# Token norms whose square roots, reciprocals and spreads go in two halves of the columns, and modulation columns and coefficients placed elsewhere

## What is computed

```python
def rms_norm(x, g):
    y = xf * lax.rsqrt(jnp.mean(xf * xf, axis=-1, keepdims=True) + EPS)
    return (y * g.astype(jnp.float32)).astype(x.dtype)
...
    mod = c_act @ ada_w[i] + ada_b[i]
    sh1, sc1, g1, sh2, sc2, g2 = [m[:, None, :] for m in jnp.split(mod, N_MOD, axis=-1)]
    h = rms_norm(x, mix_pre_g[i]) * (1.0 + sc1) + sh1
    y = hybrid_mixer(h, ...)                      # attention with forgetting, and a gated convolution
    x = x + g1 * rms_norm(y, mix_post_g[i])
    h = rms_norm(x, ffn_pre_g[i]) * (1.0 + sc2) + sh2
    y = swiglu_ffn(h, w_ffn_in[i], w_ffn_out[i])
    x = x + g2 * rms_norm(y, ffn_post_g[i])
...
    h = _modulate(x, norm_g[i], shift, scale)     # second block: a Mamba-2 mixer
    x = x + gate[:, None, :] * _mamba2_mixer(h, ...)
    hk = _modulate(x, kv_norm_g, kv_shift, kv_scale)
    ...                                           # then stick-breaking attention on keys and values of hk
    return _rmsnorm(x, final_g)
```

## Time and profile before

| | us |
|---|---|
| median of 3 runs | 1412.69 (1410.79 to 1412.97) |
| the profiled execution's own time | 1412.92 |
| its span in the trace | 1411.1 |
| TensorE busy (share of the span) | 1348.2 (96%) |
| VectorE busy | 823.5 (58%) |
| ScalarE busy | 588.5 (42%) |
| GpSimd busy | 407.2 (29%) |
| mean granted TensorE clock | 0.976 of 2.4 GHz |

### The profile page before, as it was taken

One profiled execution on the slowest core, in us unless ns is written; L12 is line 12 of the kernel. 1 busy time (PEld: TensorE's weight loads), 2 busy tenths in 40 slices (PEclk: granted clock), 3 DMA queues, 4 the chain that ended last, 5 costly groups with the idle time before them and its releaser, 6 DMA issues. The chain is left out here.

```text
span 1411.1 us, 19533 instructions
## 1 busy us (share of the span) xinstructions
PE 1348.2 (96%) x7904; PEld 1072.8 (76%) x7904; DVE 823.5 (58%) x965; ACT 588.5 (42%) x849; POOL 407.2 (29%) x191
## 2 busy tenths in 40 slices
PE   5999999799999999999999999999998999999996
PEld 3778867578888888887788876767776899777775
DVE  2789974566555564433757656778733822566544
ACT  4323656332222232113444456787522422455441
POOL 0000000149887888998100000000000050232310
PEclk9999999889999999999799999999999999999998
DMA  9434071124545536543222243334132432111121
GB/s 382 156 136 150 31 268 61 60 90 178 186 171 223 189 128 235 209 178 149 93 91 89 92 131 93 113 119 143 60 111 91 156 121 90 60 60 34 57 90 60
DMA packets 41350, 181.12 MB, mean 128 GB/s; under 512 B 3392, under 2 KB 20160, under 8 KB 21312
## 3 DMA queue, kind: packets, MB, share of 16 engines
q1 hardware_dynamic: 40128, 171.73, 33.9%
q10 hardware_dynamic: 1152, 8.39, 1.7%
HBM read 173.75 MB, written 6.36 MB: 128 GB/s over the span
## 5 line engine op out<-in xcount | busy, mean ns | idle before, releaser
L193 DVE TENSOR_TENSOR wlo<-raw,whi 128x2048 fp32r<-128x2048 f32 x95 | 257.4, 2710 | 169.2 <-ACT whi L189 166.6
L200 POOL TENSOR_TENSOR ada_raw<-ada_raw,cs 128x2048 f32<-128x2048 f32 x36 | 142.6, 3962 | 498.6 <-DVE h2lo L451 451.0
L271 PE MATMUL ps<-hhi,whi 128*128 128x512 f32 x640 | 252.1, 394 | 2.3 <-PEq L563 0.8
L271 PE MATMUL ps<-hhi,wlo 128*128 128x512 f32 x640 | 249.4, 390 | 0.0
L271 PE MATMUL ps<-hlo,whi 128*128 128x512 f32 x640 | 249.1, 389 | 0.0
L189 ACT ACTIVATE whi<-raw 128x2048 fp32r<-128x2048 f32 x95 | 181.5, 1911 | 143.6 <-PE ps L1312 91.3
L209 POOL TENSOR_TENSOR ada_raw<-ada_raw 128x1024 f32<-128x1024 f32 x72 | 166.0, 2305 | 5.6
L271 PEld LDWEIGHTS ps<-hhi,whi 128*128 128x128 f32 x640 | 120.2, 188 | 28.6 <-issue 2.4
L271 PEld LDWEIGHTS ps<-hhi,wlo 128*128 128x128 f32 x640 | 120.1, 188 | 25.6
L271 PEld LDWEIGHTS ps<-hlo,whi 128*128 128x128 f32 x640 | 120.3, 188 | 24.3
L2041 POOL TENSOR_TENSOR x<-x,rest 128x256 f32<-128x256 f32 (+3 forms) x32 | 49.0, 1532 | 160.2 <-DVE rest L2340 160.2
(11 more groups left out here) (374 smaller groups left out, 2781.1 us busy)
## 6 DMA issues: line engine op xcount, KB each, us to landing
raw<-panels SPq DMA_DIRECT2D x87, 1024.0 KB, 4.9
ada_raw<-ada SPq DMA_DIRECT2D x48, 1024.0 KB, 6.7
first<-ada SPq DMA_DIRECT2D x8, 1024.0 KB, 20.6
bc<-ac_rows SPq DMA_DIRECT2D x32, 256.0 KB, 3.7
raw<-panels ACTq DMA_DIRECT2D x8, 1024.0 KB, 5.0
x_kept<-x SPq DMA_DIRECT2D x2, 2048.0 KB, 9.7
x<-x_kept SPq DMA_DIRECT2D x2, 2048.0 KB, 7.7
x<-x_in SPq DMA_DIRECT2D x1, 2048.0 KB, 10.8
```

What stands on the lines that cost most here:

```text
L193: e.tensor_tensor(wlo[:, c % 2, :, :], raw[:, c % 2, :, :], whi[:, c % 2, :, :].bitcast(F32), ALU.subtract).then_inc(lo_split, 1)
L200: e.tensor_tensor(ada_raw[:, c % 2, :, :], ada_raw[:, c % 2, :, :], cs[:, which, :].unsqueeze(2).to_broadcast([P, KT, 256]), ALU.mult).the ...
L271: mm = e.matmul(ps[:, 2 * (qc % 2) + b, :], w[:, c % 2, 2 * k + b, :], src[part][:, k, :], **flags)
```

## The change

In `token_std` the square root is taken in two halves of the 128 columns, and so is the reciprocal in `token_rs`, each half with its own semaphore count. `spread` waits for both square roots, and then for one half's reciprocal at a time: it has 4 multiplications per half, 8 in all, whose moving operand has 64 columns. All seven norms use it. In `post2` the 13 pending columns are placed 4, 5, 1, 1, 2, 0 and not 3, 3, 1, 1, 2, 3. The two coefficients of the last block are computed at the end of VectorE's work in the Mamba part, after its fourth group's norm and ahead of the wait for `x` to come back.

```diff
+        TOKEN_HALVES = (slice(0, P // 2), slice(P // 2, P))
...
         def token_std(act, no, s, bank):
             act.wait_ge(*no("ss_used", (s + 1) * KT))
-            act.activation(rsq[:], ps[:, bank, 0:P], ACT.Sqrt, bias=eps[:, 0:1],
-                           scale=1.0 / D).then_inc(nsem["std_ready"], 1)
+            for h in TOKEN_HALVES:
+                act.activation(rsq[:, h], ps[:, bank, h], ACT.Sqrt, bias=eps[:, 0:1],
+                               scale=1.0 / D).then_inc(nsem["std_ready"], 1)
         def token_rs(dve, no, s):
-            dve.wait_ge(*no("std_ready", s + 1))
-            dve.reciprocal(rsq[:], rsq[:]).then_inc(nsem["rs_ready"], 1)
+            for i, h in enumerate(TOKEN_HALVES):
+                dve.wait_ge(*no("std_ready", 2 * s + i + 1))
+                dve.reciprocal(rsq[:, h], rsq[:, h]).then_inc(nsem["rs_ready"], 1)
         def spread(pe, no, s, bank):
-            pe.wait_ge(*no("rs_ready", s + 1))
-            for b in range(TB):
-                mm = pe.matmul(ps[:, bank, b * P:(b + 1) * P], ident[:, 32 * b:32 * b + 1].to_broadcast([P, P]), rsq[:],
-                               start=True, stop=True)
+            pe.wait_ge(*no("std_ready", 2 * s + 2))
+            for i, h in enumerate(TOKEN_HALVES):
+                pe.wait_ge(*no("rs_ready", 2 * s + i + 1))
+                for b in range(TB):
+                    mm = pe.matmul(ps[:, bank, b * P + h.start:b * P + h.stop],
+                                   ident[:, 32 * b:32 * b + 1].to_broadcast([P, P]), rsq[:, h], start=True, stop=True)
             mm.then_inc(nsem["spread"], 1)
...
+        def norm_coefs(dve, gain, sc, slot, k0=0, k1=KT):
+            dve.scalar_tensor_tensor(out=coef[:, slot, k0:k1], in0=m(sc)[:, k0:k1], scalar=1.0, in1=gain[:, k0:k1],
+                                     op0=ALU.add, op1=ALU.mult).then_inc(nsem["coef_ready"], 1)
...
-                post2 = post_norm("ffn_post", "g2", ..., last, late=(41, 54, sums, [3, 3, 1, 1, 2, 3]))
+                post2 = post_norm("ffn_post", "g2", ..., last, late=(41, 54, sums, [4, 5, 1, 1, 2, 0]))
...
                         group_rs(dve, 3)
                         norm_lo(dve, 3)
+                        norm_coefs(dve, v("kv_norm"), "kvsc", 1)
+                        norm_coefs(dve, v("norm2", KT, KT), "ssc", 2)
                         dve.wait_ge(x_back, 16)
...
                 def _(dve):
-                    pre3["coefs"](dve)
-                    pre4["coefs"](dve)
                     pre3["dve"](dve)
```

More of the change, by code:

```diff
@@ L342, in post_norm @@
             N = nsem
-            no = counting(bank_done=KT - 1, kept=KT, sq_ready=2 * KT, ss_used=2 * KT, std_ready=2, rs_ready=2, spread=2,
+            no = counting(bank_done=KT - 1, kept=KT, sq_ready=2 * KT, ss_used=2 * KT, std_ready=4, rs_ready=4, spread=2,
                           scaled=KT, x_new0=KT // 2, x_new1=KT // 2, coef_ready=1)
@@ L442, in coefs @@
             def coefs(dve, k0=0, k1=KT):
-                dve.scalar_tensor_tensor(out=coef[:, slot, k0:k1], in0=m(sc)[:, k0:k1], scalar=1.0, in1=gain[:, k0:k1],
-                                         op0=ALU.add, op1=ALU.mult).then_inc(N["coef_ready"], 1)
+                norm_coefs(dve, gain, sc, slot, k0, k1)
             def on_dve(dve, k0=0, k1=KT):
@@ L558, in build @@
             x_landed = sem("x_landed")
-            x0 = counting(sq_ready=KT, ss_used=KT, std_ready=1, rs_ready=1, spread=1)
+            x0 = counting(sq_ready=KT, ss_used=KT, std_ready=2, rs_ready=2, spread=1)
             head = pre_norm(v("mix_pre"), "sc1", "sh1", hhi, hlo, h0, ps[:, 7, :], parts=4)
@@ L1226, in build @@
                 last = co + COUNT["ffn_out"] - 1
-                post2 = post_norm("ffn_post", "g2", y_place[:, 0:KT, :], y_place[:, 8:11, :], last, late=(41, 54, sums, [3, 3, 1, 1, 2, 3]))
+                post2 = post_norm("ffn_post", "g2", y_place[:, 0:KT, :], y_place[:, 8:11, :], last, late=(41, 54, sums, [4, 5, 1, 1, 2, 0]))
                 pre2 = pre_norm(v("norm2", 0, KT), "msc", "msh", hhi, hlo, y_place[:, 11:13, :],
@@ L1440, in build @@
                 xsq = dec[:, 0:2, :, :].rearrange("p a h t -> p a (h t)")
-                no = counting(bank_done=3, x_new1=KT, sq_ready=KT, ss_used=KT, std_ready=1, rs_ready=1, spread=1)
+                no = counting(bank_done=3, x_new1=KT, sq_ready=KT, ss_used=KT, std_ready=2, rs_ready=2, spread=1)
                 M = {k: sem("m_" + k) for k in ("cols", "cols_c", "wend0", "ends", "xdt", "xw", "bt", "btok",
@@ L1987, in build @@
             pre4 = pre_norm(v("norm2", KT, KT), "ssc", "ssh", h2hi, h2lo, h0, ps[:, 7, :], slot=2)
-            fin = counting(bank_done=KT - 1, x_new1=KT, sq_ready=KT, ss_used=KT, std_ready=1, rs_ready=1, spread=1,
+            fin = counting(bank_done=KT - 1, x_new1=KT, sq_ready=KT, ss_used=KT, std_ready=2, rs_ready=2, spread=1,
                            out_ready=KT, out_stored=16 * KT)
```

## The result

| | before | after |
|---|---|---|
| median of 5 runs each, us | 1412.97 (1410.79 to 1414.84) | 1423.30 (1419.46 to 1425.59) |
| after / before | | 1.0062 [1.0047, 1.0078] |
| profiled execution, its span, us | 1412.92, 1411.1 | 1419.46, 1417.3 |
| mean granted clock in the trace | 0.976 | 0.973 |

The change makes the kernel slower by 10.3 us. The forecast was 1418.0 with a range up to 1421.0: the side was right, the size was not. The profiled execution of after is the fastest of its five runs, so its trace shows only part of the loss.

What follows compares the result with a forecast made beforehand. TensorE, busy for 96% of the span, was taken as the bound, with token norms where it stands still. Seven places summed to 5.6; +5.3 on the median 1412.69 gave 1418.0, range 1413.5 to 1421.

Steps and rivals of the forecast that it cites:

- The price of a matmul of 64 columns: In each spread, the weight load sets the price: 0.111 at 2.4 GHz, 0.214 at 1.2 GHz, eight more per norm.
- The rival that the halves cost what the whole did: At every spread, 64 columns cost half of 128, each norm wins 0.47: in all -2.7, 1410.0; chance 0.07.
- The early start: In each norm, the first half is ready for the spread at 0.94 after the square root's start, not 1.41: gain 0.47.
- The seven places: The norms' terms, first block to kernel end: 0.5 + 0.8 + 1.2 + 1.0 + 1.0 + 0.3 + 0.8 = 5.6.
- At the mixer: Two norms after the mixer: first +0.8 (+0.4 if the clock falls later), second +1.2, wholly at 1.2 GHz.
- After the feed-forward: Two norms there: first +1.0 with four `a` ahead of its spread, second +1.0 up to TensorE's next start.
- The Mamba norm: End of the Mamba part: +0.5 for the spread, -0.2 for the coefficients gone from behind it, net +0.3.
- At the end: Last norm: four matmuls start before the clock's fall, twelve behind it; VectorE at 1403.4 instead of 1402.57, +0.8.
- the lower bounds of the unseen parts: In each norm, a half reciprocal of 0.154 and square root of 0.2 give a gain near 0.98: +0.1 while warm.
- All other work of the norms moves along with them: At all seven norms, the waits that follow are on the same chain; the sum has only the norms' terms.
- The rival of the unkind clock: Projections behind norms begin at 1.2 GHz; three later returns cost 1.5 to 2.5: about 1419.5 to 1420.5; chance 0.12.
- The late sums: After the feed-forward, the 20 loads' 0.8 hold-up of the sums reaches the square root: +0.8 on top, 1418.8; chance 0.05.

Runs made afterwards that it cites:

- split_spread: Kernel before with only the spread changed, to 8 matmuls of 64 columns after a whole square root and reciprocal: 1427.35 us, ratio 1.0102 to before.
- after_noload: Kernel after without the loads of six modulation weights (`ada` 14 to 19) in the mixer: 1418.44 us, ratio 1.0026 to before.
- before_noload: Kernel before without the loads of six modulation weights (`ada` 14 to 19) in the mixer: 1411.90 us, ratio 0.9981 to before.
- head_halves: Kernel before with the first block's norm alone in halves: 1416.56 us, ratio 1.0020 to before.
- head_whole: Kernel after with the first block's norm whole, the other six in halves, columns and coefficients moved: 1421.62 us, ratio 1.0052 to before.

## Why the prediction was off in size

**The price of a matmul of 64 columns: right.** The loads stand 0.111 apart at full clock ((1.86 - 0.19) / 15) and 0.211 at half, and `split_spread` shows the doubled spread costs 1.60 at a cold norm. The rival that the halves cost what the whole did is dead: by it `split_spread` would have cost nothing. The rule of the Trainium skill, page "TensorE: Matmul & The Clock Gate", Part 1, section "Wait — 56ns, not 53.3ns?", by which the moving columns set the distance, does not describe these multiplications: 64, 128 and one column all stand 0.111 apart here, each behind a weight load of its own.

**The early start: a little too large.** Half a square root and half a reciprocal had the length taken, but at the mixer's norms the first load starts 1.02 behind the square root and the first matmul 1.05 (272.05 - 271.00), not 0.94: between the end of the first half's reciprocal and the first load lie 0.12 (271.91 to 272.02), where 0.05 was taken. The gain is 0.36 to 0.40 and not 0.47 a norm. No hole opened in the middle of the 16, as foreseen.

**The seven places: right as a whole, in part by luck.** Forecast 5.6, found 0.6 + 2.1 + 1.3 + 0.2 + 0.6 = 4.8 as a mean over four traces of each. At the mixer the square root to VectorE grew by 0.61 (forecast 0.8) and 1.21 (1.2), in the first trace of after. After the feed-forward the forecast was 0.7 too high for the stage, but 0.3 too low up to the projection (2.3); the clock's earlier return behind it hid that, and no term of the sum stood for it. The Mamba norm's +0.24 (3.34 - 3.10) up to the scaled tile stands beside +0.3, and the coefficients did cost nothing in their new place. At the end it is +0.45 on the chain where 0.8 was said. The 6.5 between `after_noload` and `before_noload` is near the local sum too, but the trace of `after_noload` has the fall near 942 and that of `before_noload` has not, so it is no clean measure of it.

The sum itself has slips. With starts 0.111 apart from 269.44, the tenth of the 16 is at 270.44 and the eleventh at 270.55, still ahead of the fall, so five follow and not six: +0.6, which is what was measured. At the end of the kernel five start before the fall and not four, again +0.6. And at the lower bounds of the unseen parts a gain of 0.98 against a price of 0.89 is -0.1 a norm, not +0.1.

**The step that failed** is the sum itself: it put everything outside the norms at nothing ("All other work of the norms moves along with them"), and took the clock for something that the norms meet, not for something that can be lost elsewhere. In the mixer the clock falls after TensorE's wait for modulation weights in each of the six traces whose first norm starts its spread early and in four of ten others, at 3.7 to 5.4 each time; that is +2.0 between the four traces of each kernel, and taking the loads away takes 2.8 off the distance. Behind the start of the first projection, from 28.4 to 34.4, it is +0.9 as a mean, by a longer rest at half clock, and outside the span 0.3. Between 814 and 990 it is 1.7 to 1.8 in two of four traces of after, by a fall that a kernel unchanged up to there had as well. The rival of the unkind clock (0.12) had the direction, but its price was for returns behind a norm, 1.5 to 2.5 in all. From the first projection matmul behind a norm to the end of its stage the traces show, as means, +0.9 in the first block, +0.2 at the mixer, -0.95 after the feed-forward and +0.3 at the Mamba norm: some +0.4 together. Its sum, 1419.5 to 1420.5, was still too low, because no fall outside the norms was counted. The late sums may have cost something: the square root of the second norm starts 13.93 behind the first's in after (669.52 to 683.45) and 12.48 in before, 1.45 more, of which the first norm's own chain explains 1.36 (square root to VectorE 4.04 against 2.68, forecast +1.0). That leaves 0.1 for them, so this rival was no part of the miss.

**What stays open.** That the fall in the mixer costs about 4 us when it happens is shown. Why a first norm with an early spread has it every time is not: 6 of 6 against 4 of 10 is a strong leaning and no mechanism. A mere delay upstream does not decide it: from 34.4 to 186 all traces agree within 0.06, and from 17.0 to 34.4 those with the fall are -0.1 to 2.4 longer than the first trace of before, those without it 0 to 2.4. How a change in the first norm would become a longer wait for a transfer was not tried. `head_halves` has a median of only +2.7, and six of its eleven runs lie between 1414.98 and 1416.56, so the fall is probably not in every one of them; and `head_whole` is still 7.7 slower with no fall in the mixer in its trace, but one behind the feed-forward. Nor is it settled what brings the fall near 947 in some executions, or whether the +0.9 from 28.4 to 34.4 comes from the change: traces with a whole first norm range from -0.1 to 1.5 there.

## What to carry to other kernels

Cutting a small multiplication in two to start it earlier pays only if its price falls with the number of moving columns; where each has a weight load of its own, look at the distance of the loads in the trace, since here that distance was the same for 1, 64 and 128 columns. A local sum, however well it is worked out, can be too low where some stretch elsewhere is close to losing the clock: list the places where TensorE waits a microsecond or more for a transfer, and ask what a shift by half a microsecond upstream does there. Take several traces of each kernel before judging a stage, because this one has a stage with two lengths 4 us apart in the unchanged kernel as well. And split a stage where the next dense work begins: what the chain costs and what the clock gives or takes behind it are two sizes, and after the feed-forward they had opposite signs (+2.3 and -0.95).

## What the runs showed of the hardware

Float32 weight loads of 128x128 for a matmul of 64 columns stood 0.111 us apart at 2.4 GHz and 0.211 at 1.2 GHz, as with 1 and 128 columns. A reciprocal of 128x64 float32 took 0.494 to 0.554 where one of 128x128 took 0.953, and a square root 0.31 where the whole took 0.37, so halving the square root saves almost nothing. And an execution lost 4 us at once, with the clock at half for 6.8 us, where TensorE had waited twice for weights between stretches of small matmuls: of four traces of the kernel before, the two that had waited 2.6 together lost it, and the two that had waited 1.5 and 1.9 kept the full clock. The longest single wait in after was 1.5, and the clock fell all the same.
